# Expert weights of a mixture-of-experts layer: a fourth place for gate matrices, loaded before the first turn, and another order of the experts with two turns

## What is computed

```python
def _moe(h, router_w, router_bias, w_gate, w_up, w_down):
    x = h.reshape(B * T, D)
    probs = jax.nn.softmax(jnp.einsum('nd,de->ne', x, router_w).astype(f32), axis=-1)
    ...
    _, local = lax.top_k(sel_in, TOP_K)
    expert = grp[:, None] * EXP_PER_GROUP + local
    ...
    hid = jax.nn.silu(jnp.einsum('nd,edf->nef', x, w_gate)) * jnp.einsum('nd,edf->nef', x, w_up)
    y = jnp.einsum('nef,efd->nd', hid * gates[..., None], w_down)
```

## Time and profile before

| | us |
|---|---|
| runs: median, lowest, highest of 3 | 1501.41, 1495.56, 1515.63 |
| the profiled execution's own time | 1497.87 |
| its span, first to last instruction | 1496.1 |
| turns of layer 0 (601.26 to 863.27) | 262.01 |
| turns of layer 1 (1209.38 to 1460.79) | 251.41 |
| TensorE matmul busy in the span | 1275.3 (85%) |

### The profile page before, as it was taken

One profiled execution on the slowest core, in us unless ns is written; L12 is line 12 of the kernel. 1 busy time (PEld: TensorE's weight loads), 2 busy tenths in 40 slices (PEclk: granted clock), 3 DMA queues, 4 the chain that ended last, 5 costly groups with the idle time before them and its releaser, 6 DMA issues.

```text
span 1496.1 us, 17316 instructions
## 1 busy us (share of the span) xinstructions
PE 1275.3 (85%) x6005; PEld 721.0 (48%) x6005; DVE 461.8 (31%) x1139; ACT 295.4 (20%) x622; POOL 323.5 (22%) x328
## 2 busy tenths in 40 slices
PE   3979999999996994989898758999999669987873
PEld 1447767766775654333333225666665523322321
DVE  0454555465543124000000044434332500100004
ACT  2234323332331121100000031111111200100001
POOL 0041223132211000333332102131320023332210
PEclk9979999999996895999998979999999679999997
DMA  9755535562554026698999862342410759999973
GB/s 383 302 203 210 214 89 182 199 207 72 217 195 152 4 103 283 259 355 300 419 390 428 358 248 97 108 145 89 146 49 16 288 233 391 355 429 427 427 329 136
DMA packets 91695, 352.99 MB, mean 236 GB/s; under 512 B 29136, under 2 KB 66832, under 8 KB 72592
## 3 DMA queue, kind: packets, MB, share of 16 engines
q0 software_dynamic: 20160, 188.77, 30.8%
q1 hardware_dynamic: 70144, 163.11, 29.9%
q10 hardware_dynamic: 1360, 0.71, 0.2%
HBM read 376.04 MB, written 21.60 MB: 266 GB/s over the span
## 4 chain that ended last, share of the span: by engine, by line
PE 68%; DMA 20%; DVE 5%; issue 2%; ACT 2%; SPq 1%; POOL 0%; POOLq 0%; DVEq 0%; ACTq 0%
DMA slot<-in_w_x,widx 14%; PE bank L1792 10%; PE bank L1267 10%; PE bank L663 8%; PE bank L1831 7%; PE bank L1187 6%; PE bank L744 3%; PE bank L345 3%; PE bank L671 2%; DMA slot<-in_ada_w 2%; PE bank L780 2%; PE bank L713 2%; PE bank L724 2%; PE bank L410 2%; PE bank L1591 1%
## 5 line engine op out<-in xcount | busy, mean ns | idle before, releaser
L1792 PE MATMUL bank<-slot,scr 128*64 128x512 f32 x1216 | 286.4, 629 | 37.0 <-DMA slot<-in_w_x,widx 35.3
L1792 PEld LDWEIGHTS bank<-slot,scr 128*64 128x64 f32 x1216 | 92.2, 145 | 228.3 <-issue 174.0
L1267 PE MATMUL bank<-hnT,slot 128*128 128x384 f32 x512 | 169.5, 488 | 3.5 <-DMA slot<-in_mlstm_w 2.1
L1831 PE MATMUL bank<-slot,scr 128*64 128x512 f32 x608 | 139.5, 612 | 26.4 <-DMA slot<-in_w_x,widx 19.0
L1267 PEld LDWEIGHTS bank<-hnT,slot 128*128 128x128 f32 x512 | 95.6, 190 | 67.4 <-DMA slot<-in_mlstm_w 2.3
L663 PE MATMUL bank<-hnT,slot 128*128 128x384 f32 x384 | 126.0, 488 | 0.0
L1934 POOL DMA_INDIRECT slot<-in_w_x,widx x102 | 102.3, 1003 | 60.7 <-POOL widx L1930 42.6
L1896 DVE TENSOR_TENSOR scr<-scr,bank 128x512 f32<-128x512 f32 x19 | 13.1, 687 | 307.0 <-PE bank L1792 307.0
L663 PEld LDWEIGHTS bank<-hnT,slot 128*128 128x128 f32 x384 | 72.3, 190 | 55.2 <-issue 6.5
L1831 PEld LDWEIGHTS bank<-slot,scr 128*64 128x64 f32 x608 | 46.9, 141 | 106.7 <-issue 91.0
L1187 PE MATMUL bank<-yT,slot 128*128 128x384 f32 x256 | 84.7, 493 | 0.7 <-DVE yT L1449 0.7
(11 more groups left out here) (283 smaller groups left out, 1681.2 us busy)
## 6 DMA issues: line engine op xcount, KB each, us to landing
slot<-in_ada_w SPq DMA_DIRECT2D x24, 2048.0 KB, 13.4
slot<-in_w_x SPq DMA_DIRECT2D x12, 2048.0 KB, 12.8
slot<-in_gdn_w SPq DMA_DIRECT2D x9, 2048.0 KB, 15.1
slot<-in_mlstm_w SPq DMA_DIRECT2D x16, 1024.0 KB, 6.9
scr<-rows_d SPq DMA_DIRECT2D x32, 384.0 KB, 4.3
slot<-in_w_out SPq DMA_DIRECT2D x2, 4096.0 KB, 15.4
slot<-inverse_d SPq DMA_DIRECT2D x16, 384.0 KB, 4.1
slot<-out_d SPq DMA_DIRECT2D x6, 1024.0 KB, 7.0
```

The costliest lines, as they stand in the source:

```text
L1267: mm = nc.tensor.matmul(bank[:, PROJ_BANK[s], 0:T], slot[:, 0, (s * KD + k) * P:(s * KD + k + 1) * P], hnT[:, k, :], start=(k == 0), stop= ...
L1792: mm = nc.tensor.matmul(bank[lanes[lane], m, :], xgT[:, k * P + lane * CAP:k * P + (lane + 1) * CAP], w_of[m][lane][:, k, :], start=(k == ...
L1831: mm = nc.tensor.matmul(bank[lanes[lane], 5 + h, :], hidT[:, k * P + lane * CAP:k * P + (lane + 1) * CAP], w_of[W_DOWN][lane][:, k, h * 51 ...
```

## The change

Three things change, in both layers.

1. `hnT`, `yT` and `scr` become one tensor `wide`, and its first 2 x 4096 columns are `spare`: a fourth pair of weight places, over `hnT`, `yT` and the first 2048 columns of `htok`. GpSimd loads the gate pair of turn 1 there right after it has issued the gather of turn 0. Turn 1 then reads its gate matrices from `spare`, and the gate places in `slot`, which turn 0 sets free, are loaded for turn 2 at once. Turn 1 thus issues no gate load, and from turn 2 on all goes as before. Since `slot` doesn't hold turn 1's matrices, the gate pair of turn 2 is loaded in full even where a lane keeps its expert: `full_at` holds the rows of the expert at work (a scan carries it over kept turns).
2. Turn 1 is written out on TensorE and on GpSimd; the loops begin at turn 2.
3. The keys of experts with several turns change (3.0 to 4.0, and `C_MULTI`). By these inputs, a lane now keeps its expert in turns 3, 5, 6 and 8 of layer 0, and in turns 3 and 5 of layer 1. The number of turns and of matrices stays what it was.

```diff
-    c[:, C_MULTI:C_MULTI + E] = e // PER_LANE - 1.5 - e % PER_LANE
+    c[:, C_MULTI:C_MULTI + E] = 2 * (e // PER_LANE) - 1.5 - e % PER_LANE
...
-        hnT = sb("hnT", [P, KD, T])
-        yT = sb("yT", [P, KD, T])
+        SCR = 11520
+        wide = sb("wide", [P, 2 * KD * T + SCR])
+        hnT = wide[:, 0:KD * T].rearrange("p (k t) -> p k t", t=T)
+        yT = wide[:, KD * T:2 * KD * T].rearrange("p (k t) -> p k t", t=T)
+        scr = wide[:, 2 * KD * T:2 * KD * T + SCR]
+        spare = wide[:, 0:LANES * SLOT].rearrange("p (l n) -> p l n", l=LANES)
...
-            step(STT(out=late_key, in0=seen, scalar=3.0, in1=const[:, C_MULTI:C_MULTI + E], op0=ALU.mult, op1=ALU.add))
+            step(STT(out=late_key, in0=seen, scalar=4.0, in1=const[:, C_MULTI:C_MULTI + E], op0=ALU.mult, op1=ALU.add))
...
-            nc.vector.tensor_scalar(load_f[1], load_f[0], 0.0, float(FAR), ALU.is_equal, ALU.mult)
+            step(nc.vector.tensor_scalar(load_f[1], load_f[0], 0.0, None, ALU.is_equal))
+            step(nc.vector.tensor_tensor_scan(held_f, load_f[1], load_f[0], 0.0, ALU.mult, ALU.add))
+            nc.vector.tensor_scalar(full_at[:, :, :], held_f.rearrange("p (l n) -> p l n", l=LANES)[:, :, 0:3], 3.0 * P,
+                                    const[:, C_ROW + layer:C_ROW + layer + 1], ALU.mult, ALU.add)
+            nc.vector.tensor_scalar(load_f[1], load_f[1], float(FAR), None, ALU.mult)
...
             def gate_up(it):
                 pe.wait_ge(e["xg"], 2 * it + 2)
-                weights(W_GATE, "gate_in", it)
-                product(it, W_GATE, e["gate"])
+                if isinstance(it, int) and it == 1:
+                    pe.wait_ge(spare_in, 32 * layer + 32)
+                    product(w_spare, W_GATE, e["gate"])
+                else:
+                    weights(W_GATE, "gate_in", it if isinstance(it, int) else it - 1)
+                    product(w_of[W_GATE], W_GATE, e["gate"])
...
             turn(0, False)
-            with pe.Fori(1, n - 1) as it:
+            turn(1, True)
+            with pe.Fori(2, n - 1) as it:
...
                 wait_turn(pool, e["gate"], it + 1, e_route, 6 * layer + 6)
-                load(it + 1, W_GATE, e["gate_in"], it * IDX + 3)
+                if isinstance(it, int) and it == 0:
+                    load_of([slot[:, 2 * W_GATE + lane, :] for lane in range(LANES)], full_at[:, :, 2],
+                            W_GATE, e["gate_in"], at)
+                elif not isinstance(it, int):
+                    load(it + 1, W_GATE, e["gate_in"], it * IDX + at)
...
             gather(0, 1)
+            load_of([spare[:, lane, :] for lane in range(LANES)], full_at[:, :, 1], W_SPARE, spare_in, 2)
             pool.wait_ge(e["xp"], 1)
-            gather(1, 2)
+            gather(1, 3)
             turn(0, False, True)
-            with pool.Fori(1, n - 2) as it:
+            turn(1, True, True)
+            with pool.Fori(2, n - 2) as it:
                 turn(it, True, True)
```

More of the change, by code:

```diff
@@ L211, in program @@
         hcol = sb("hcol", [P, 4, NU])
-        SCR = 11520
-        scr = sb("scr", [P, SCR])
         at = [0]
@@ L1579, in program @@
                  for lane in range(LANES)] for m in range(3)]
+        w_spare = [spare[:, lane, :].rearrange("p (k n) -> p k n", k=KD) for lane in range(LANES)]
+        W_SPARE = 3
         def turns(eng, layer):
@@ L1787, in moe_pe, with product @@
             lanes = [slice(lane * CAP, (lane + 1) * CAP) for lane in range(LANES)]
-            def product(it, m, done):
+            def product(w, m, done):
                 for k in range(KD):
@@ L1927, in gather, with load_of, load @@
                                              bounds_check=T - 1, oob_is_err=False).then_inc(e["got"], 16)
-            def load(it, m, landed, count):
-                nc.gpsimd.tensor_copy(widx[:, m, :], load_at[:, m, :, bass.ds(it, 1)].rearrange("p l n -> p (l n)"))\
-                    .then_inc(e["idx"], 1)
+            def load_of(dst, rows, m, landed, count):
+                nc.gpsimd.tensor_copy(widx[:, m, :], rows).then_inc(e["idx"], 1)
                 ready(count)
                 for lane in range(LANES):
-                    nc.gpsimd.indirect_dma_start(slot[:, 2 * m + lane, :], None, a["w_x"],
+                    nc.gpsimd.indirect_dma_start(dst[lane], None, a["w_x"],
                                                  bass.IndirectOffsetOnAxis(ap=widx[:, m, lane:lane + 1], axis=0),
                                                  bounds_check=DEPTH * E * 3 * P - 1, oob_is_err=False).then_inc(landed, 16)
+            def load(it, m, landed, count):
+                load_of([slot[:, 2 * m + lane, :] for lane in range(LANES)],
+                        load_at[:, m, :, bass.ds(it, 1)].rearrange("p l n -> p (l n)"), m, landed, count)
             def scatter(it, count):
@@ L1944, in turn @@
             def turn(it, again, more):
+                at = 3 if not isinstance(it, int) else 4 - it
                 wait_turn(pool, e["gate"], it + 1, e_route, 6 * layer + 6)
[L1946 removed]
+                if isinstance(it, int) and it == 0:
+                    load_of([slot[:, 2 * W_GATE + lane, :] for lane in range(LANES)], full_at[:, :, 2],
+                            W_GATE, e["gate_in"], at)
+                elif not isinstance(it, int):
+                    load(it + 1, W_GATE, e["gate_in"], it * IDX + at)
                 wait_turn(pool, e["up"], it + 1, e_route, 6 * layer + 6)
[L1948 removed]
+                load(it + 1, W_UP, e["up_in"], it * IDX + at + 1)
                 if more:
                     wait_turn(pool, e["xp"], it + 2, e_route, 6 * layer + 6)
[L1951 removed]
+                    gather(it + 2, it * IDX + at + 2)
                 wait_turn(pool, e["y_ps"], it + 1, e_route, 6 * layer + 6)
[L1953 removed]
+                load(it + 1, W_DOWN, e["down_in"], it * IDX + at + 2 + more)
                 if again:
```

12 lines of the change are left out of this document (7 added, 5 removed).

## The result

The changed kernel took 1478.85 us (median of 4 runs, 1475.18 to 1487.8) beside 1502.16 for the kernel before (4 runs). The ratio is 0.9872, with a 95% interval of 0.9834 to 0.991 (the two medians by themselves give 0.9845). So the changed kernel is faster by 1.3%, less than the 2% line, as forecast; 1477.0 had been predicted. Its profiled execution took 1478.17, 19.7 less than that of before (1497.87).

A forecast was written before the change was run, and what follows sets the result against it. DMA engines bound full turns behind full ones, TensorE the waitless turns. A gain of 22.6 us from the turns less 0.6 for routing is 22.0; off 1497.87 that is 1475.9, given as 1477, range 1464 to 1496.

The forecast's parts named there:

- Full behind light: Expert stages: a full turn after a light or first one waits only for its up or down pair; 27.9 us.
- Full behind full: Expert stages: a full turn after a full one is bound by the DMA engines; 31.2 us.
- Waitless: Expert stages: a turn that waits for no weights takes TensorE's own time, 23.0 us.
- Turn 1 gets nothing: Turn 1, both layers: up and down loads stand as before, so it keeps its 29.0 and 27.5 us.
- my 22.6: Both expert stages: summed gain from turns priced by kind, 10.2 us in layer 0 and 12.4 in layer 1.
- Turn 2, the narrow place: Turn 2: down pair lands 12.0 us after issue, 1.4 us before needed; turn costs 23.0; a miss costs 0 to 3.
- The last turn of layer 0: Layer 0's last turn: now behind a light turn, 26.7 us instead of 30.0, taking 3.3 off.
- The routing: Before the token lists: three small VectorE instructions more, partly hidden; cost 0.3 us a layer, 0.6 in all, bounds 0 to 1.4.
- The gather of turn 0: Ahead of turn 0: still 6 and 10 us; rival (10%): the pair delays it 9.8 us a layer, 1495.5.
- Neither part would do alone: Early pair alone saves only where TensorE doesn't wait; new order alone leaves turn 2 full behind full at 31.2 us.
- Instruction loads: Rival (5%): GpSimd's moved loop loads instructions at each return, 4.2 us for each of 11 turns, 46 us, giving 1522.
- more is gained: Rival (15%): waits and low clock in full turns shrink once the stream is ahead; 8.8 us more, 1467.1, down to 1465.

The follow-up runs named there:

- the experiment with the exchanged lines: The changed kernel with the early pair issued ahead of turn 0's gather instead of behind it; ratio to the kernel before 0.9965.
- the changed kernel's third trace: The changed kernel unaltered, run again on another chip as the measure for two experiments; ratio to the kernel before 0.9816, stages 496.3 us.
- the later timings: The changed kernel run twice more, unaltered, against the kernel before on the same chip; ratios 0.9805 and 0.9816.

## Why the prediction was right, point by point

- **The price of turns by kind: right.** Full behind light, forecast 27.9: 27.7, 26.9, 28.7, 27.9. Full behind full, 31.2: 31.0. Waitless, 23.0: 23.0 in layer 0's turns 2, 3, 5, 6 and 8.
- **Turn 1 gets nothing: right**, but not at a fixed size. 31.3 us in layer 0 instead of 29.0; the kernel itself repeats this turn at 31.3, 27.9 and 31.0, and the one before at 29.0 and 30.8. In the long ones its down product waits 3.8 to 4.8 us for its weights and then runs at a lower granted clock, 9.6 to 10.1 us; in the changed kernel's short one it waits 1.7 and takes 7.1. The prediction had no term for that. This was 2.3 of the 5.5 us by which the two stages fell short of my 22.6 in the first pair of traces.

```profile
650.17 9.63 PE L1846 MATMUL bank<-slot,wide 128*64 128x512 f32 x32 [4.75 <-DMA slot<-in_w_x,widx]
```

- **Turn 2, the narrow place: mis-sized.** "It fits by 1.4 us" held in two of three traces of layer 0 and in none of layer 1, where TensorE waited 2.03 us for the down pair (0.74 of it is there anyway) and the turn took 24.3, 24.4 and 23.7. The step that failed is the landing of 12.0 us on an idle queue: in layer 1 the queue wasn't idle, since turn 1 had been shorter (27.6 us) and the gather ahead landed only at 1259.56; the pair's second DMA, issued at 1255.44, took 14.6 and landed at 1270.06. I had kept 0 to 3 us for it, and it cost 1.3. The step used layer 0's rows alone, though turn 1 of layer 1 had been 27.5 us before. And where it held, luck had a part: of the six times that the three traces show, the down pair was there in time in the two where turn 1 took 31.3 and 31.0 us, and late in the four where it took 27.6 to 28.0.

```profile
1270.19 7.09 PE L1846 MATMUL bank<-slot,wide 128*64 128x512 f32 x32 [2.03 <-DMA slot<-in_w_x,widx]
```

- **The last turn of layer 0: mis-sized.** 28.1 in all three traces instead of 26.7. I had taken 3.3 us off a last turn behind a full one; what goes is its gate wait (3.24 us, and the slow gate product of 8.78 behind it). The up wait stays and grows from 1.00 to 2.73 us, and now the up product is the slow one (8.78 instead of 7.09).
- **The routing: at most what was priced.** From SyncE's first load to the gather's issue 41.8 us before in layer 0; 42.0, 42.0 and 40.5 after. Layer 1 shows no cost (40.5 and 40.6, then 39.0, 40.0 and 39.8).
- **The gather of turn 0: right**, as its times above show, and the experiment with the exchanged lines shows that this came from the order of issue. The second gather landed at 611.19, some 8 us before it was needed.
- **"Neither part would do alone": right for the pair** (1.0019). For the order it was half right: turn 2 did take 31.0, yet the order by itself was worth 7.5 to 10.8 us, since it takes away two full-behind-full turns in each layer and puts one back, turn 2. By my own prices that is 6.2 us (260.0 and 247.2 against 262.0 and 251.4), which I hadn't written out.
- **The rivals.** Instruction loads: four packets on the instruction queue in 300 us (three before; five in the changed kernel's third trace), loop turns of 23.0 us. Nothing. Of "more is gained", the later timings (28 us) are nearly there, but not by its mechanism: the turns kept their prices, and the surplus over the stages' 19.9 us lies in the 3.7 us between the stages, which no step of the prediction has (2.7 of them with TensorE's clock in the mixer).

The sum was 22.0 us. Measured are 19.9 for the stages on the means, 24.4 from the first load to the end, and 19, 29 and 28 by the three timings. That the first pair of traces came out 19.7 us apart, so near to 22.0, is in part luck: their stages gave 17.1, and 4.1 came from between the stages, less 1.7 ahead of them.

## What to carry to other kernels

Where a queue of transfers is the bound in some turns and idle in others, sort turns by what stands ahead of them and price each kind from the trace; then ask of a change which turn's kind it alters. Moving a load into an idle stretch is worth its duration only if the load is taken from a turn where somebody waits, so here the hoist was worth nothing by itself, the reordering 8 to 11 us, and both together 20. And whatever the compute engine waits for goes into the queue ahead of the bulk.

## What the runs showed of the hardware that was not expected

The part of the program ahead of the change has the same instructions in all kernels, and it ended anywhere between 544.0 and 558.3 us over fourteen traces. That spread is more than half of the change's gain and about as large as that of single runs of one kernel. Much of it is TensorE's clock: its busy time in this part goes from 481.0 to 492.8 us, and its granted clock from 0.95 to 0.92. Not all of it: the longest, 558.3, had 488.4. Comparing traces from the first instruction that a change touches took most of this away (945.8 and 948.6; 924.6, 921.0, 922.9).

A small gather that TensorE waits for took 3.5 and 4.6 us with free DMA engines, 6 and 10 beside another queue's bulk loads, and 12 and 16 behind 4.2 MB in its own queue. A wait of 11.4 us also left TensorE at a lower granted clock for the next product (9.91 us instead of 7.09).
